# A table of slots for the side steps, and a phase's sums read by two engines

## The reference

```python
def peer_ffn(h, w_q, sub_keys, expert_u, expert_v):
    ...
        best_s, best_pos = lax.top_k(cand_s, PEER_TOPK)
        idx = jnp.take_along_axis(cand_i, best_pos, axis=-1)
        gate = jax.nn.softmax(best_s, axis=-1)
        u = expert_u[idx]
        act = jax.nn.gelu(jnp.einsum('nhkd,nd->nhk', u, xb, preferred_element_type=jnp.float32), approximate=False)
        coef = (gate * act).astype(xb.dtype)
        return jnp.einsum('nhk,nhkd->nd', coef, expert_v[idx])

for layer in range(DEPTH):
    h = h + mix.astype(h.dtype)          # mix = mixer(rmsnorm(h))
    ffn = peer_ffn(rmsnorm(h, ffn_norm[layer]), ...)
    h = h + ffn.astype(h.dtype)
```

## Time and profile before

| | |
|---|---|
| Median of 3 runs | 1704.35 us (1704.04 to 1709.86) |
| The profiled execution's own time | 1712.91 us |
| Its span in the trace | 1711.1 us |
| Busy: PE, VectorE, ScalarE, GpSimd | 1230.4, 1195.4, 484.9, 602.0 us |
| Moved by DMA | 670.19 MB |

### The profile page before, as it was taken

The page is one execution under the profiler, slowest core; times in us unless marked ns, Lnnn a source line. Parts: engine busy times, 40 slices in busy tenths (PEclk is TensorE's granted clock), DMA queues, the critical chain, the costliest instruction groups (busy, mean ns, idle before and its releaser), DMA issues.

```text
span 1711.1 us, 21732 instructions
## 1 busy us (share of the span) xinstructions
PE 1230.4 (72%) x7384; PEld 593.8 (35%) x7384; DVE 1195.4 (70%) x3389; ACT 484.9 (28%) x1123; POOL 602.0 (35%) x525
## 2 busy tenths in 40 slices
PE   6865886757849978968695699696869656645554
PEld 2453232215516744422361376342226311111111
DVE  3356678766586888885755688889665787777755
ACT  0122124212213544621232244363112222222211
POOL 1023424433332322334233233331433444455451
PEclk9987888888967989979896699897989866787786
DMA  8579999999998999989999799998999999999995
GB/s 302 197 302 423 382 423 418 422 422 395 424 421 315 424 421 408 395 325 425 422 422 422 305 420 421 422 411 341 381 423 422 420 421 421 422 421 421 422 421 242
DMA packets 84076, 670.19 MB, mean 392 GB/s; under 512 B 9376, under 2 KB 9520, under 8 KB 10624
## 3 DMA queue, kind: packets, MB, share of 16 engines
q0 software_dynamic: 74608, 540.65, 76.8%
q1 hardware_dynamic: 9216, 127.65, 17.9%
q10 hardware_dynamic: 144, 0.52, 0.1%
HBM read 667.74 MB, written 1.05 MB: 391 GB/s over the span
## 4 chain that ended last, share of the span: by engine, by line
DMA 34%; PE 30%; DVE 22%; issue 7%; ACT 4%; POOL 2%; ACTq 0%; DVEq 0%; POOLq 0%; SPq 0%; PEldq 0%
DMA ring<-in_experts,idx 32%; PE acc L737 13%; PE act_bank L485 10%; DVE ring L1272 7%; PE dve_bank L471 3%; DVE scratch L931 3%; DMA wbuf<-in_weights 2%; POOL ring L428 2%; DVE h L1293 1%; DVE onehot L931 1%; PE act_bank L718 1%; ACT scratch L772 1%; ACT diag L898 1%; PE act_bank L471 1%; ACT L772 1%
## 5 line engine op out<-in xcount | busy, mean ns | idle before, releaser
L428 POOL DMA_INDIRECT ring<-in_experts,idx x512 | 596.0, 1164 | 1061.8 <-PE acc L737 853.0
L737 PE MATMUL acc<-ring,diag 64*64 64x512 f32 x4096 | 642.3, 757 | 332.8 <-ACT diag L898 318.7
L1272 DVE CUSTOM_DVE_ANT_0 ring<-ring,hn 128x1024 f32<-128x1024 f32 x512 | 622.7, 1224 | 265.0 <-DMA ring<-in_experts,idx 247.1
L737 PEld LDWEIGHTS acc<-ring,diag 64*64 64x64 f32 x4096 | 160.2, 160 | 721.6 <-ACT diag L898 466.2
L891 ACT ACTIVATE acts<-dots 128x2 f32<-128x2 f32 x256 | 52.0, 203 | 775.1 <-DVE dots L1272 752.0
L485 PE MATMUL act_bank<-hnT,wbuf 128*128 128x128 f32 x2048 | 255.7, 283 | 15.6 <-ACT hnT L772 10.9
L485 PEld LDWEIGHTS act_bank<-hnT,wbuf 128*128 128x128 f32 x2048 | 242.5, 197 | 60.0 <-issue 57.6
L898 ACT ACTIVATE diag<-cst,coefs 128x64 f32<-128x64 f32 x512 | 150.3, 340 | 204.8 <-DVE coefs L1280 173.5
L1280 DVE TENSOR_TENSOR coefs<-acts,gate 128x2 f32<-128x2 f32 x256 | 41.4, 162 | 96.9 <-ACT acts L891 86.3
L772 ACT ACT_TABLE_LOAD x77 | 98.8, 1283 | 11.7 <-DMA rowc<-in_rows 9.6
L471 PE MATMUL dve_bank<-wbuf,scratch 128*128 128x512 f32 x192 | 94.5, 628 | 1.0 <-ACT scratch L772 0.7
(11 more groups left out here) (125 smaller groups left out, 834.0 us busy)
## 6 DMA issues: line engine op xcount, KB each, us to landing
wbuf<-in_weights SPq DMA_DIRECT2D x60, 2048.0 KB
ring<-in_experts,idx POOLq DMA_INDIRECT x512
scratch<-in_bias POOLq DMA_DIRECT2D x1, 1024.0 KB, 11.3
out<-h SPq DMA_DIRECT2D x2, 512.0 KB
scratch<-in_bands POOLq DMA_DIRECT2D x1, 768.0 KB, 6.5
h<-in_x SPq DMA_DIRECT2D x1, 512.0 KB, 3.9
gains<-in_gains POOLq DMA_DIRECT2D x1, 512.0 KB, 4.9
h<-in_x POOLq DMA_DIRECT2D x1, 512.0 KB, 18.1
```

Of the source, the lines that this page charges most:

```text
L428: pool.indirect_dma_start(ring[:, n % RING], None, io[f"experts{layer}"], bass.IndirectOffsetOnAxis(idx[:, at:at + 1], 0),).then_inc(sem(f ...
L737: last[rows] = pe.matmul(acc[rows][half][home:home + HALF_P], diag[part, n % DIAGS], ring[part, slot, D + half * CW:D + (half + 1) * CW], ...
L1272: dve.tensor_tensor_reduce(out=ring[:, slot, 0:D], in0=ring[:, slot, 0:D], in1=hn[:, phase % NBLK], scale=1.0, scalar=0.0, op0=ALU.mult, o ...
```

## The change

1. `ON_THE_WAY` and its shares are replaced by `SIDE_SLOTS`: for each layer a list of (slot, tick), counted from slot `FIRST_SIDE` = 4 of the phase (from slot 14 in phase 0). Ticks between two entries are still spread evenly. VectorE and ScalarE take no side steps in slots 0 to 3. The queries end at slot 121 instead of 112.
2. Consumers get a tick, and in the table a slot, of their own behind their producers: `norm` yields between the mean square and the scaling; the waits `emptied(...)` move from behind the transposes to the step that needs them; the four groups of `y` transposes go two and two, and VectorE empties each two a tick later than PE writes them; ScalarE's and VectorE's shares of `queries` move a tick back.
3. The sums of a phase: VectorE adds the even slots' sums straight from the banks at slot 2 (`add_even`, four additions), ScalarE copies the odd slots' sums to `odd_sums` at slot 1 behind its diagonals (`copy_odd`, four copies), and VectorE adds these at slot 3 (`add_odd`, one addition of 128 x 1024). PE waits at slot 2 for both. The last phase keeps eight additions.
4. `ROUTE_LEAD` is 20 instead of 24: each part of a route stands four slots later.

```diff
-T_OUT1 = T_YT + 3
+T_OUT1 = T_YT + 4
...
-MIXED_BY, ASKED_BY = 92, 112
+ASKED_BY = 121
...
-ON_THE_WAY = (((T_OUT0, 0.65),), ((T_CB, 0.38), (T_YT, 0.68)))
-KNOTS = [(0, T_EARLY + 1), (QUERIED_BY, START[1])]
+SIDE_SLOTS = (
...
+    ((0, 0.5), (3, 1), (5, 2), (6, T_IN1 - 2), (9, T_IN1 - 1), (10, T_IN1), (40, T_IN1 + 32), (46, T_CB), (51, T_SCAN),
...
+FIRST_SIDE = GROUP + 2
...
-ROUTE_LEAD, ROUTE_STEP = 24, 3
+ROUTE_LEAD, ROUTE_STEP = 20, 3
...
                 transposes(hn[:, b, 0:4 * P], 4, kind)
                 transposes(hn[:, b, 4 * P:8 * P], 4, kind)
-                emptied(kind)
...
-                yield T_YT
-                lane.need("y_ready")
                 for c in range(4):
+                    if c % 2 == 0:
+                        yield T_YT + c
+                        if c == 0:
+                            lane.need("y_ready")
                     transposes(y[:, c * CW:(c + 1) * CW], 4, "dve")
...
                     if n == GROUP and phase:
                         pe.wait_ge(sem("acc_read"), phase)
+                        pe.wait_ge(sem("odd_copied"), phase)
...
+            def copy_odd(phase):
+
+                for rows in range(2):
+                    act.wait_ge(sem(f"pairs_summed{rows}"), (phase + 1) * STEPS * GROUPS + AHEAD)
+                for half in range(2):
+                    for rows in range(2):
+                        part = slice(rows * HALF_P, (rows + 1) * HALF_P)
+                        home = slice((1 - rows) * HALF_P, (2 - rows) * HALF_P)
+                        started = lane.start(act.activation(odd_sums[part, half * CW:(half + 1) * CW],
+                                                            acc[rows][half][home], ACT.Copy))
...
-                    beside.upto(pace(phase, n))
+                    if n >= FIRST_SIDE or not phase:
+                        beside.upto(pace(phase, n))
...
+                    if n == GROUP - 1 and phase:
+                        copy_odd(phase - 1)
...
                 mean_square(b, hn[:, b])
+                yield 0.6
                 ts(hn[:, b], h[:, b], stat[:, 32:33], None, ALU.mult)
...
-                    yield T_YT + 1 + c // 2
+                    yield T_YT + 1 + c // 2 * 2
...
+            def add_even(phase):
+
+                all_summed(phase)
+                for half in range(2):
+                    for rows in range(2):
+                        part = slice(rows * HALF_P, (rows + 1) * HALF_P)
+                        out = h[part, phase % NBLK, half * CW:(half + 1) * CW]
+                        started = lane.start(dve.tensor_tensor(out, out, acc[rows][half][part], ALU.add))
+                lane.after(started)
                 lane.tell("acc_read")
+
+            def add_odd(phase):
+
+                lane.need("odd_copied")
+                tt(h[:, phase % NBLK], h[:, phase % NBLK], odd_sums, ALU.add)
...
                     if n == GROUP and phase:
-                        add_experts(phase - 1)
+                        add_even(phase - 1)
+                    if n == GROUP + 1 and phase:
+                        add_odd(phase - 1)
```

More of the change, by code:

```diff
@@ L523, in mixer0 @@
                     yield T_IN0 + 4 * c
+                    if c == 0:
+                        emptied("dve")
                     if c == 3:
@@ L704, in queries @@
                     yield at
+                    if hd == 0:
+                        emptied("act")
+                        pe.sem_inc(sem("hn_transposed"), 1)
                     if hd % 2 == 0:
@@ L900, in make_diagonals @@
                 ins.then_inc(sem("diag_ready"), 1)
+            def copy_odd(phase):
[8 more added lines that the diff above has]
+                lane.after(started)
+                lane.tell("odd_copied")
             def experts(phase, beside, routes):
```

50 lines of the change are left out of this document (29 added, 21 removed).

## The result

| | before | after |
|---|---|---|
| median of the runs | 1705.51 us (4 runs, 1704.04 to 1709.86) | 1686.49 us (4 runs, 1683.25 to 1688.72) |
| profiled execution, span | 1711.1 us | 1686.8 us |
| mean GB/s over the span | 392 | 397 |

The ratio is 0.9883, 95% interval [0.9855, 0.9911]: the change makes the kernel 1.2% faster. 1663 us were forecast, with a range of 1645 to 1685, so the direction was right and the size was not: the spans differ by 24.3 us, the medians by 19.0, and 41.2 were forecast.

The account below looks back on a forecast made before the run. DMA was taken as the bound, with at most 56.6 us to regain. Terms 20.2 + 16.3 + 2.9 + 2.0 = 41.4 us of the profiled 1712.91, taken as 41.2 off the 1704.35 median, gave 1663 us, range 1645 to 1685.

Parts of the forecast that it names:

- What bounds the kernel: Nearly the whole span: DMA bound at 422 GB/s, so only DMA's underused time, 56.6 us at most, can come back.
- Starts of phases 1 and 2: First slots of both phases: holes of 10.9 and 12.3 us shrink to 1.5 us each, 20.2 us back.
- One sign: Near the starts of phases 1 and 2: GB/s above 410 in every 40 us if the forecast is right.
- Smaller holes: At 170-190 us (norm) and 400-420 us (transposes in queries): 2.9 and 2.0 us back.
- What costs nothing: Later routes, output-projection chunks every 12.5 us and ScalarE's 2.4 us of copies: no cost; PE waits some tenths for chunks.
- That sign named for "wrong": PE waiting for wbuf, the weight chunks' buffer, would show the forecast wrong; no size given.
- The rival on the slower side: Output projection: late chunks hold PE and the ring; 1723 us if a chunk takes 20 us; chance 0.04.
- Transposes of `y` and scans: Later part of phases 1 and 2: PE's bank waits go, VectorE's overrun leaves 3 and 7 us; 16.3 us back.
- the light slots behind (80 to 88): Behind the scan: with gathers in flight they absorb part of phase 2's 11 us overrun, leaving 7 us.
- the signs named for "wrong": Among them a gap between gathers of 10 us or more behind slot 98 or 76, where VectorE's list is longest.
- VectorE takes it back: Phases 1 and 2: moved steps collide with routes, about 10 and 13 us stay lost, 1679 us; chance 0.20.
- the fourth term: The sum's 16.3 us for the transposes of y and scans: 10.8 in phase 1 and 5.5 in phase 2.

Follow-up runs that it names:

- routes_clear: Changed kernel with the routes of phases 1 and 2 due at slots -20, -12, -5, 13, 21, 30, 38 and 86, clear of scan and start; 1669.78 us.
- sums_only: Kernel before with the shared sums alone, side steps starting one slot later at their old pace; 1704.92 us (0.9991).
- sums_on_vector: Changed kernel with all eight additions of a phase's sums back on VectorE, no ScalarE copies, tables as changed; 1688.53 us (0.9896).
- y_in_one_go: Changed kernel with the sixteen transposes of y in one step again; 1692.75 us (0.9921).
- out_relaxed: Changed kernel with layer 1's output projection over 18 slots instead of 12, queries later over 20 slots, routes 14 slots ahead instead of 20; 1689.21 us (0.9903).

## Why the prediction was right in its direction and wrong in its size

- **What bounds the kernel.** Right, and the most useful part: lost DMA time fell by 24.9 us and the span by 24.3. It also holds for the experiments: the best kernel loses 11.5 us in phases 0 to 2 (changed: 32.3) and its span is 18.8 shorter.
- **Starts of phases 1 and 2.** Right: 20.2 forecast, 20.5 measured. First pair sum at 507.7 forecast and 505.19 measured, which is 2.94 us behind the start of the additions ("some 3 us"); copies 4 x 0.61 us (four of "about 0.6"); gathers at 509.74 and 516.79 for 511.5 and 519. One sign was missed by a little: 510 to 550 us is at 406 GB/s, not above 410. That the sums are not what matters there was the reading of the earlier trace rows against the earlier trace rows, and `sums_only` (0.9991) and `sums_on_vector` (0.9896 for 0.9883) bear it out.
- **Smaller holes.** 4.9 forecast, 4.1 measured, in part by luck: both places lose nothing any more (421 and 423 GB/s), and 1.8 us are lost newly at 290 to 310 us and 1.6 at 320 to 340.
- **What costs nothing.** The chunks: right in what they cost, not in the wait. TensorE waited for `wbuf` 7.3 us in all of phases 1 and 2, 2.3 at most, where it had waited 0.2 before and "some tenths" were forecast. That sign named for "wrong" showed, and yet the output projection loses nothing once the routes stand elsewhere (`routes_clear` waits 6.7 us for `wbuf`). The rival on the slower side had no part in it. Of GpSimd's waits, one alone ended with VectorE's numbers, the first of the kernel (77.6 us), so that routes four slots later cost no gather anything, as argued.
- **Transposes of `y` and scans: the step that failed.** "I leave 3 us in phase 1 and 7 in phase 2" was 13.6 and 13.3. So 0.1 us came back where 16.3 were forecast, and it lies under the forecast's own lower bound of about 9 (by its figures 26.3 less overruns of 12.0 and the present 4.1, which is 10.2). Its parts: (a) PE's wait for banks went, as said, worth 4.0 us in phase 1 and 1.1 in phase 2 (`y_in_one_go`: 6.3 us in time). But TensorE also waits for `y_ready`, 7.28 and 6.21 us, where no wait beyond 3 was forecast. (b) VectorE's busy time in the 24 slots was forecast at 72.6 and 82.2 us and measured at 73.12 and 79.49. (c) It was turned into time "at the 90% that VectorE reaches at its densest": 80.7 and 91.3. Phase 2 took 88.8, but phase 1 took 86.6, at 84%. The steps there wait for TensorE and ScalarE and for each other, and there is no single share at which VectorE is full: the convolution of `routes_clear` has it at 99.01 of 110.76 us (89%) and loses nothing. (d) The sum ended at the 24 slots. The stretch ahead (slots 44 to 55) loses 2.2 us in phase 1, those behind (79 to 98) 3.5 and 6.4, slots 98 to 107 another 0.6 and 3.0. That "the light slots behind (80 to 88) take a part" was wrong in its sign: TensorE has its blocks and chunks there, and what the scan was late by came back as holes. This is also where the signs named for "wrong" showed: gathers 10.4 us apart behind slot 76 and 12.1 behind slot 98, at places that do lose DMA time.
- **The cause.** The routes on top of the side steps of slots 44 to 98. With all other steps left where they are and the routes of two phases laid around the scan, both phases behind their starts lose 5 us together and not 27, and the time falls from 1686.5 to 1671.0 us. The forecast named this as its rival "VectorE takes it back", with 10 and 13 us kept, and weighed it at 0.20, with "the slots from which the work was taken were no lighter" against it. (The rival's price is off in its own sum: 10 and 13 kept in place of 3 and 7 is 13 us, not 16. The 16 is all of the fourth term, which is what was measured: 41.2 - 16 = 25.2 for the 24.3 us of the spans.) It should have been the forecast: by its own tables the change put all between the scan and the queries into 21 slots of each phase, where it had 29, and it moved the routes by four slots only.

The gain by the medians (19.0 us) is smaller than by the spans (24.3), since the profiled execution of before was 7 to 9 us over its median and that of after 2. So of the 22.2 us that the medians fall short of the 41.2, some 5 are the long execution that the lost time was read from, and 17 are the terms of the sum; the rival's 1679 is short of 1686.5 for the same reason.

## What to carry to other kernels

Where an in-order engine serves a ring of transfers and a schedule of side work, sum its load slot by slot over everything that it is given, and go on with the sum past the dense stretch until the lateness is paid back; a mean busy share says neither where it is late nor whether it loses. When a table moves one stream of work, the second stream (here the routes) has to be moved with it: the first alone gave 1.2%, both 2.1%, the second alone lost 0.8%. Sharing a reduction between two engines is worth what the engine lacks at that place, here nothing that could be told with free slots around it and half a per cent by the medians in a crowded start, of which the traces explain less than half.

## What the runs showed of the hardware

- VectorE and ScalarE read the same four banks at the same time without slowing each other: four additions in 2.83 us (0.71 each, as when VectorE reads alone in the earlier trace rows), four copies in 2.44 us (0.61 each). The forecast allowed for up to twice that for the copies. They read opposite halves of the partitions of each bank. The Trainium skill (Advanced Engine Details and Errata, Bank Collisions) says that the two can read at full speed at once if they don't meet in one bank and partition; by that rule, the trace agrees. In `out_relaxed` ScalarE begins 1.33 us ahead of VectorE in phase 2, so that two of its copies are over before VectorE reads at all, and the four take the same time:

```profile
930.77 2.44 ACT L926 ACTIVATE scratch<-acc 64x512 f32<-64x512 f32 x4
932.10 2.83 DVE L1327 TENSOR_TENSOR h<-h,acc 64x512 f32<-64x512 f32 x4
```

- A copy of 64 x 512 takes ScalarE 0.61 us from one to the next, no less than the 593 ns of 128 x 512 in the earlier trace rows: half the partitions save nothing.
- ScalarE's change of function table takes 1.28 us, and the exponential behind it starts at once (504.76 and 506.05). The Trainium skill (ScalarE: Activation LUTs, What ACT_TABLE_LOAD costs) has a drain of about 1380 ns on top, 2.66 us in all; this trace doesn't show it. By the profile ScalarE loads a table 80 times at L788 (exponentials, SiLU, a logarithm), 102.6 us, and 68 times ahead of the GELU, 87.2 us.
- The Trainium skill (DMA: Bandwidth & Descriptors, Where 436 GB/s comes from) has about 358 GB/s, a memory stack's 716 over its two cores, as the ceiling for such transfers. This kernel runs on one core, and every undisturbed stretch of its runs is at 417 to 426, so the rows decide, as in the forecast; no run here has a second core at work.
- VectorE at 89% over 110 us cost the DMA queue nothing (423 GB/s), while at 69% over 40 us, with waits for other engines between its steps, the queue fell to 263 GB/s.
